# A two-block transformer forward on one core: activation tiles 512 columns apart, working-area regions at multiples of 128 columns

## The reference, cut to what matters

```python
def reference(x, ctx, ...):
    for l in range(2):                                   # first block
        hx = modulate(rmsnorm(x, norm_w[l]), ...)
        hc = modulate(rmsnorm(xc, norm_w[l]), ...)
        px = split_proj(hx @ w_in[l])                    # 1024 x 11008
        pc = split_proj(hc @ w_in[l])                    # layer 1: only ret_k, ret_v, att_k, att_v
        # four branches: retention, short conv, conformer conv, windowed attention, each (256, 512)
        merged = sum(sigmoid(g) * (br @ w_branch[i]) for i, (g, br) in enumerate(...))
        x = x + gate_x * (merged @ w_out[l])             # and xc likewise in layer 0
    x = rmsnorm(x, final_norm_w)
    for i in range(2):                                   # second block
        h = rmsnorm_2(x, norm_g[i, 0]) * (1 + sc_m) + sh_m
        y = rglru_mixer(h, ...) if i == 0 else gla_mixer(h, ...)
        x = x + gt_m * rmsnorm_2(y, norm_g[i, 1])
        h = rmsnorm_2(x, norm_g[i, 2]) * (1 + sc_f) + sh_f
        u = causal_dwconv(h @ w_up[i], conv_w, conv_b)   # 1024 x 5632
        g, val = split(u)
        x = x + gt_f * rmsnorm_2((gelu(g) * val) @ w_down[i], norm_g[i, 3])
    return x
```

## Time and profile before

| | |
|---|---|
| median of three runs | 1770.68 us (1768.67 to 1771.08) |
| span of the profiled execution | 1766.0 us; 4.7 us less than the median, and no other time of this execution is on record |
| TensorE busy | 1717.7 us (97%) |
| VectorE busy | 1400.0 us (79%) |
| ScalarE busy | 873.9 us (49%) |
| HBM traffic over the span | 170 GB/s, 50.6% of the DMA engines' time |

### The profile page before, as it was taken

How to read it: one execution, slowest core, us unless ns; L and a number is a source line. 1 busy time by engine, 2 the same in 40 slices (tenths; PEclk the granted TensorE clock), 3 DMA queues, 4 the chain that set the end, 5 groups by cost and what they waited for, 6 DMA issues and landing times.

```text
span 1766.0 us, 29817 instructions
## 1 busy us (share of the span) xinstructions
PE 1717.7 (97%) x11416; PEld 1526.8 (86%) x11416; DVE 1400.0 (79%) x2572; ACT 873.9 (49%) x1542; POOL 0.2 (0%) x4
## 2 busy tenths in 40 slices
PE   6999999999999999999999999999999999999998
PEld 3788887777888888897988899999999999999998
DVE  7799996546789998888877699977888568778874
ACT  4222224456233233353346755577666547566553
POOL 0000000000000000000000000000000000000000
PEclk9999999999999999999999999999999999999999
DMA  9583211211767876744323289744455545345553
GB/s 342 203 282 118 85 63 49 96 37 37 253 224 244 276 243 215 238 144 143 120 96 101 94 307 320 252 156 156 160 190 172 189 135 159 115 143 192 191 173 114
DMA packets 242188, 301.42 MB, mean 171 GB/s; under 512 B 6000, under 2 KB 223472, under 8 KB 241664
## 3 DMA queue, kind: packets, MB, share of 16 engines
q1 hardware_dynamic: 242048, 299.52, 50.6%
HBM read 298.45 MB, written 1.05 MB: 170 GB/s over the span
## 4 chain that ended last, share of the span: by engine, by line
PE 46%; DVE 5%; ACT 3%; issue 2%; DVEq 0%; ACTq 0%
PE bank L667 10%; PE bank L662 10%; PE bank L664 10%; PE bank L1044 3%; PE bank L1045 3%; PE bank L1046 3%; ACT w_hi L1359 1%; DVE w_lo L2116 1%; PE bank L638 1%; PE bank L640 1%; PE bank L639 1%; PE bank L1109 1%; PE bank L1175 1%; PE bank L1014 1%; PE bank L1160 1%
## 5 line engine op out<-in xcount | busy, mean ns | idle before, releaser
L2116 DVE TENSOR_TENSOR w_lo<-ring,w_hi 128x1024 fp32r<-128x1024 f32 (+2 forms) x436 | 489.4, 1131 | 182.4 <-ACT w_hi L1359 181.0
L1359 ACT ACTIVATE w_hi<-ring 128x1024 fp32r<-128x1024 f32 (+2 forms) x436 | 423.7, 982 | 166.9 <-PE bank L667 99.4
L662 PE MATMUL bank<-h_hi,w_hi 128*128 128x256 f32 (+2 forms) x2142 | 386.6, 322 | 0.4
L667 PE MATMUL bank<-h_hi,w_lo 128*128 128x256 f32 (+2 forms) x2142 | 379.1, 319 | 0.1
L664 PE MATMUL bank<-h_lo,w_hi 128*128 128x256 f32 (+2 forms) x2142 | 379.0, 319 | 0.0
L662 PEld LDWEIGHTS bank<-h_hi,w_hi 128*128 128x128 f32 x2142 | 316.6, 189 | 35.5 <-issue 2.7
L667 PEld LDWEIGHTS bank<-h_hi,w_lo 128*128 128x128 f32 x2142 | 317.0, 188 | 30.1 <-DVE w_lo L2116 0.3
L664 PEld LDWEIGHTS bank<-h_lo,w_hi 128*128 128x128 f32 x2142 | 317.1, 188 | 29.9
L1345 ACT ACTIVATE work<-bank 128x512 f32<-128x512 f32 (+1 forms) x134 | 67.3, 521 | 255.8 <-PE bank L667 205.4
L1345 ACT ACTIVATE arena<-bank 128x256 f32<-128x256 f32 (+4 forms) x125 | 56.4, 454 | 205.3 <-PE bank L667 125.4
L2423 DVE SCALAR_TENSOR_TENSOR arena<-arena,params 128x512 f32<-128x512 f32 (+1 forms) x240 | 130.5, 612 | 0.0
(11 more groups left out here) (324 smaller groups left out, 2286.4 us busy)
## 6 DMA issues: line engine op xcount, KB each, us to landing
ring<-in_w_in SPq DMA_DIRECT2D x86, 1024.0 KB, 5.4
arena<-in_ada_w_t SPq DMA_DIRECT2D x96, 512.0 KB, 6.0
ring<-in_ffn_w_up SPq DMA_DIRECT2D x44, 1024.0 KB, 5.0
ring<-in_w_branch SPq DMA_DIRECT2D x32, 512.0 KB, 4.7
arena<-in_w_mod_t SPq DMA_DIRECT2D x32, 512.0 KB, 5.3
ring<-in_ffn_w_down SPq DMA_DIRECT2D x16, 1024.0 KB, 5.1
ring<-in_gla_w_in SPq DMA_DIRECT2D x12, 1024.0 KB, 5.2
ring<-in_w_out SPq DMA_DIRECT2D x8, 1024.0 KB, 6.1
```

Of the source, the lines that this page charges most:

```text
L662: pe.matmul(out[:, 0:n], w[0][:, k, :], hi(k, n), start=k == 0, stop=False)
L667: m = pe.matmul(out[:, 0:n], w[1][:, k, :], hi(k, n), start=False, stop=k == tiles - 1)
L1359: nc.scalar.activation(w_hi[u % PARTS][:, 0:src.shape[1], :], src, ACT.Copy)\
L2116: step(nc.vector.tensor_tensor(w_lo[u % PARTS][:, 0:nk, :], src, w_hi[u % PARTS][:, 0:nk, :].bitcast(F32), ALU.subtract), f"lo {u}", *(["u ...
```

## The change

The tiles of h_hi and h_lo are 512 columns apart for every stage and start at column 0; both_hi and both_lo go away, because they are now the same as h_hi and h_lo. g_hi and g_lo start at column 0 of a tile and so reach two columns into the tile's second half; the merged sums of layer 1, which lay in that half, move to the arena (columns 0 and 6400). The arena regions that lay 16 columns short of a multiple of 128 (2288, 4336, ...) or 16 above one (16656) go to multiples of 128, x1_hi, x1_lo and the slots of the modulation blocks move by 16 columns, and the arena grows from 18,704 to 18,816 columns. The two h tensors shrink by 128 columns each, so that everything behind them lies up to 256 columns lower. On all engines the instructions stand in the same order with the same shapes, and the waits are the same; only addresses differ, and for the merged sums of layer 1 also the tensor.

```diff
--- before.py
+++ after.py
@@ -153,12 +153,10 @@
         params, tables = sbuf("params", N_PARAM), sbuf("tables", N_TABLE)
         xT = sbuf("xT", KT * 2 * S)[:].rearrange("p (t s) -> p t s", t=KT)
 
-        h_parts = [sbuf(n, KT * (2 * S + 16), F32R)[:].rearrange("p (t s) -> p t s", t=KT) for n in ("h_hi", "h_lo")]
-        h_hi, h_lo = (h[:, :, 16:16 + 2 * S] for h in h_parts)
-        g_hi, g_lo = (h[:, :, 14:14 + LATE_N] for h in h_parts)
-        both_hi, both_lo = (h.rearrange("p t s -> p (t s)")[:, 0:KT * 2 * S].rearrange("p (t s) -> p t s", t=KT)
-                            for h in h_parts)
-        in_hi, in_lo = (both_hi, h_hi), (both_lo, h_lo)
+        h_parts = [sbuf(n, KT * 2 * S, F32R)[:].rearrange("p (t s) -> p t s", t=KT) for n in ("h_hi", "h_lo")]
+        h_hi, h_lo = h_parts
+        g_hi, g_lo = (h[:, :, 0:LATE_N] for h in h_parts)
+        in_hi, in_lo = (h_hi, h_hi), (h_lo, h_lo)
 
         w_parts = [sbuf(n, PARTS * KT * P, F32R)[:].rearrange("p (u t n) -> p u t n", u=PARTS, t=KT) for n in ("w_hi", "w_lo")]
         w_hi, w_lo = ([w[:, i] for i in range(PARTS)] for w in w_parts)
@@ -190,7 +188,7 @@
         level = tables[:, at:at + LATE]
         gla_a = tables[0:16, at + LATE:at + LATE + 512]
 
-        arena_cols = 18704
+        arena_cols = 18816
 
         with nc.sbuf_tensor("arena", [P, arena_cols], F32) as arena:
             pass
@@ -214,33 +212,34 @@
         u_pad = carve(0, BT, 2, S + 2 * PAD), carve(BT * (S + 2), BT, 1, S + 2 * PAD)
         k_wt = [carve(1024 * i, ST, HEADS, P) for i in range(2)]
         att_o = carve(0, BT, 2 * S)
-        s_br = carve(2288, BT, 2 * S)
-        f_br = carve(4336, BT, 2 * S)
-        ret_q = ret_o = carve(6384, BT, 2 * S)
-        ret_k, ret_v = carve(8432, BT, 2 * S), carve(10480, 2 * ST, BW)
-        att_q = carve(12528, BT, 2 * S)
-        z_sil = dict(ret=carve(8432, BT, 2 * S), att=carve(10480, BT, 2 * S), cf=carve(12528, BT, 2 * S))
-        merged = carve(8432, KT, 2 * S)
-        att_k, att_ks = carve(14576, 2 * S), carve(15088, 2 * S)
-        att_v = carve(15600, 2 * ST, P)
-        state = carve(16112, HEADS, 2, P)
+        s_br = carve(2304, BT, 2 * S)
+        f_br = carve(4352, BT, 2 * S)
+        ret_q = ret_o = carve(6400, BT, 2 * S)
+        ret_k, ret_v = carve(8448, BT, 2 * S), carve(10496, 2 * ST, BW)
+        att_q = carve(12544, BT, 2 * S)
+        z_sil = dict(ret=carve(8448, BT, 2 * S), att=carve(10496, BT, 2 * S), cf=carve(12544, BT, 2 * S))
+        merged = carve(8448, KT, 2 * S)
+        att_k, att_ks = carve(14592, 2 * S), carve(15104, 2 * S)
+        att_v = carve(15616, 2 * ST, P)
+        state = carve(16128, HEADS, 2, P)
         branch = dict(ret=ret_o, sc=s_br, cf=f_br, att=att_o)
 
         def merged_part(l, lo, k):
 
             if l:
-                return (h_lo if lo else h_hi)[:, k, S:2 * S]
+                at = (0, 6400)[k // 4] + 2 * S * (k % 4) + S * lo
+                return arena_r[:, at:at + S]
             if k < 6:
-                at = (0, 2288, 6384)[k // 2] + 4 * S * (k % 2) + 2 * S * lo
+                at = (0, 2304, 6400)[k // 2] + 4 * S * (k % 2) + 2 * S * lo
                 return arena_r[:, at:at + 2 * S]
-            return (both_lo if lo else both_hi)[:, k, :]
+            return (h_lo if lo else h_hi)[:, k, :]
 
 
         def parts_of(at):
             return arena_r[:, at:at + BT * 2 * S].rearrange("p (t s) -> p t s", t=BT)
 
-        branch_hi = parts_of(16656)
-        z_sil["sc"] = carve(16656, BT, 2 * S)
+        branch_hi = parts_of(16768)
+        z_sil["sc"] = carve(16768, BT, 2 * S)
 
         def z_part(l, a, n):
 
@@ -248,7 +247,7 @@
                 return z_sil[a][:, n, :]
             return f_br[:, n, S:2 * S] if a == "sc" else z_sil[a][:, n, 0:S]
 
-        branch_lo = dict(ret=parts_of(6384), sc=parts_of(2288), cf=parts_of(4336), att=parts_of(0))
+        branch_lo = dict(ret=parts_of(6400), sc=parts_of(2304), cf=parts_of(4352), att=parts_of(0))
 
         def merged_tile(l, n):
 
@@ -263,7 +262,7 @@
             return early_gate(m) if l and m < EARLY_GATES else act_t[m % 4][:, 0:2 * S if l == 0 else S]
 
         x1_hi, x1_lo = (arena_r[:, c:c + KT * LATE_N].rearrange("p (t s) -> p t s", t=KT)
-                        for c in (8432, 8432 + KT * LATE_N))
+                        for c in (8448, 8448 + KT * LATE_N))
 
         def row_of(i):
 
@@ -456,7 +455,7 @@
         mod_slot_of = {m: i for i, m in enumerate(mod_order)}
 
         def mod_slot(m):
-            return carve(12560 + D * (mod_slot_of[m] % MOD_SLOTS), D)
+            return carve(12576 + D * (mod_slot_of[m] % MOD_SLOTS), D)
 
         def mod_in(m):
 
@@ -1483,7 +1482,7 @@
                     split_to(2)
                     shift_row(1)
                     shift_col(1)
-                    modulated("n1 0", (0, 1), lambda k, g: mod1[0][:, k, g:g + 1], start_shift, both_hi)
+                    modulated("n1 0", (0, 1), lambda k, g: mod1[0][:, k, g:g + 1], start_shift, h_hi)
                 if l:
                     act.wait_ge(shapes_landed, 32)
 
@@ -2247,7 +2246,7 @@
                     dve.wait_ge(x_landed, 32)
                     inverse("n1 0", 2 * S)
                     tile, low = normed("n1 0", (0, 1), lambda k, g: gain1[0][:, k, g:g + 1], lambda k, g: mod1[0][:, k, g:g + 1],
-                                      both_hi, both_lo)
+                                      h_hi, h_lo)
                     after(f"start mod {START + 1}")
                     modulation1(0, 0, 4)
                     split_to(1)
```

## The result

The changed kernel took 1775.84 us (median of five runs, 1775.33 to 1777.55), the kernel before 1768.74 us beside it (five runs, 1767.47 to 1771.08). That is 1.0040 of the time before, interval 1.0028 to 1.0052: 7.1 us slower. The forecast was 1779.5 us against a median before of 1770.68, so +8.9. Three of the five runs before are those that the prediction had; two more brought their median from 1770.68 to 1768.74.

A forecast was written before the change was run, and what follows sets the result against it. TensorE's matmul pace, set by operand addresses, was taken as the bound. 11.9 + 1.8 - 3.8 - 1.0 = +8.9 us gave a forecast of 1779.5 us, range 1766 to 1785.

The forecast's parts named there:

- 256 columns, streamed and down with h: Projections, 4,752 matmuls, 117.5 to 120.0 ns, +11.9 us; down projections with h stationary, 1,056, 118.3 to 120.0, +1.8 us.
- 512 columns: Arena matmuls in layer 0, 231.3 to 226.8 ns; layer 1's early tiles, 231.9 to 226.8; together -3.8 us.
- 258 columns: Late stages, 312 matmuls whose offsets change: -1.2 to +0.8 us, taken as 0.
- absorbed by waits: TensorE's two waits for a weight tile's high part absorb 0 to 4.3 us of the loss; 1.0 taken.
- the first witness: Down projection's middle part with arena operands, already at offset 0: 33 matmuls of 256 columns at 120.0 ns each.
- the second: Low part of att_o at offset 0: four matmuls at 117.5 ns, after eight at offset 16 at 113.8.
- the fast pace: 256 columns at 113.8 ns, seen in eight matmuls at offset 16 and lost within four at offset 0.
- 256 columns find the fast pace: Rival: 256 columns settle near 113.8 ns at offset 0, 26 us gained, 1744 us; chance 0.11.
- half of it: Rival: pace wanders after stalls, short groups stay near 118.7 ns, +2.7 us, 1773 us; chance 0.09.
- the 312 matmuls of one group: The 258-column matmuls (104 x 3) in late stages; each could gain 3.7 ns or lose 2.5.
- the waits for w_hi: TensorE's waits for a weight tile's high part, 1.7 and 2.6 us, where part of the loss might be absorbed.
- The 4.7 us between them: Median 1770.68 us above the profiled span of 1766.0; added to the predicted span 1774.9 to give 1779.6.

The follow-up runs named there:

- experiment 1: Matmuls alone in place of the whole computation, start column and tile distance varied, two orders: 256 columns 119.9 ns at offset 0, 113.3 and 117.9 at 16.
- experiment 4: Matmuls alone again, 256 columns at every fourth offset, 512 at every eighth, weights also starting at 16 or 48: 113.3 to 120.0 ns for 256 columns.
- experiment 5: Changed kernel with h 48 columns later from layer 1 on, ff_hi and ff_lo from 9808, merged sums partly from 6448: 1759.25 us, ratio 0.9942.
- the arena alone: Kernel before with only the arena's regions moved to multiples of 128 and 2 KB less scratch: 1767.12 us, ratio 0.9994 (0.9985 to 1.0002).

## Why the prediction was right

Direction, mechanism and most of the size were right. The 11,416 matmuls stand in the same order in both traces, so each one's distance to the next can be compared one by one. The sums over the span, beside the terms predicted (where a matmul belongs to a pace and where to a wait is a choice that moves some tenths of a microsecond between rows):

| term | predicted | measured |
|---|---|---|
| 256 columns, streamed and down with h | +11.9 +1.8 = +13.7 | +12.45 (6,079 matmuls) |
| 512 columns | -3.8 | -3.58 |
| 258 columns | 0 (-1.2 to +0.8) | +0.30 |
| absorbed by waits | -1.0 (0 to 4.3) | -0.68 |
| plain float32 matmuls | not named | -0.49 |
| stretches at half clock, with the waits they shorten | not named | +1.78 |
| sum over the span | +8.9 | +9.7 |

- **256 columns.** The pace at offset 0 is 120.0 wherever it settles, as the first witness had it; the second had shown only that the fast pace is lost there. The term is 1.2 us too large because the pace before was not 117.5 everywhere: its mean over all was 117.86 and after it 119.91, and the 6,079 include the 288 of the down projection's arena part, which had 120.0 before as after (eight stretches of 36, not of 39). The rival "256 columns find the fast pace" fell (120.0, never 113), and so did "half of it" (113.8 became 120.0 in the merge). The first witness streams its operand in two pieces and the second had only four matmuls, at 117.5 and not yet at 120.0, so neither proved the pace of a projection; that they held was partly luck. The runs bear them out afterwards: in experiments 1 and 4 offset 0 had one pace in every series (120.0 and 226.7), where 16 and 48 had two, and experiment 5 shows that the two-piece stream follows its offset too.
- **The word "offset".** That it is the difference of the two operands' columns, and not one operand's column, was assumed; experiment 4 shows it (both at 16 or at 48 runs as both at 0). That it counts modulo 128 was wrong: modulo 64. It changed nothing here, since 112 and 16 and 0 are told apart by both.
- **512 columns.** All three places came to 226.7; -3.58 against -3.8.
- **258 columns.** 120.15 to 120.68 ns, +0.30 us, inside the bounds, though these were worked out for the 312 matmuls of one group, and the trace has 576: those of the other lines and those from the arena were left out.
- **Absorbed.** Little, as said, but elsewhere: not at the waits for w_hi, which hardly moved, but before output tiles in layer 1's early projections, where the loop of ScalarE and VectorE sets the cadence (an output tile every 3.15 us in both kernels). From 768 to 800 us both kernels went through the same matmuls in 32.0 us, though those of 256 columns had gone from 117.9 to 119.7 ns. One wait grew (0.98 to 1.43 us before the last merged sums).
- **Not foreseen: stretches at half clock.** One window of 4 us in the kernel before, at 1.00 (it had 1.00 from 802 to 806 us as well), and two in the changed one and in the one with the arena alone:

```profile
41.00:45.00 4.00, 4.00 (x19) 2.54 (x18) 2.81 (x6) 2.65 (x5) 0.00 (x0) 1.00 1.10 351
```

```profile
41.00:45.00 4.00, 4.00 (x13) 3.06 (x11) 2.81 (x6) 2.63 (x5) 0.00 (x0) 0.59 1.10 353
802.00:806.00 4.00, 4.00 (x12) 3.17 (x11) 4.00 (x10) 0.00 (x0) 0.00 (x0) 0.57 0.05 12
```

```profile
41.00:45.00 4.00, 4.00 (x16) 2.55 (x15) 3.37 (x6) 1.40 (x3) 0.00 (x0) 0.83 1.09 353
802.00:806.00 4.00, 4.00 (x16) 3.17 (x15) 4.00 (x9) 0.00 (x0) 0.00 (x0) 0.81 0.39 89
```

The mean granted clock is 0.59 and 0.57, the 1.2 GHz level for most of the window, and 13 matmuls run where 19 did at 1.00. Before the second, TensorE had waited 1.9 us. It is not the change's doing as far as shown: the kernel with the arena alone, with h as before and no slower than before, has such stretches in the same two places. They cost the profiled execution 1.8 us net: a wait of TensorE at 60 us became 1.3 us shorter, which gave back most of the 1.6 that the first one had cost. Every run has a mean granted clock on record, and these speak for chance: 0.997 in the profiled execution of the kernel before, but 0.994 to 0.997 in 16 later runs of it, only three of them at 0.997; 0.995 and 0.996 in the five runs of the changed kernel.
- **From the span to the median.** The 4.7 us between them were carried over as they stood, and this step was wrong. Every run on record with both has 1.8 us between time and span (1777.55 and 1775.7 for the profiled one of the changed kernel). So the profiled execution of the kernel before was one of about 1767.8 us, 2.9 faster than the median that stood beside it, and these 2.9 are the larger part of the forecast's 3.7 us too much. The same explains 9.7 in the spans against 7.1 in the medians: the changed kernel's profiled execution was the slowest of its five (1775.7, their median span 1774.1), and that of the kernel before lay 0.9 us below its own median. The terms that the forecast named came to +8.5 against its +8.9; that this is so near is in part luck, because the first was 1.2 too large and the others together 0.8 too small. The other 1.3 us of the spans are terms that it didn't name.

The Trainium skill was weighed in the prediction: by "SBUF — State Buffer", section "SBUF: two separate sides", TensorE never waits on anyone, and by "TensorE: Matmul & The Clock Gate", section "Step-by-step: what each phase is for", loading the next weights takes nothing from the running matmul. By the prediction's reading of these, addresses would cost nothing. The runs disagree with that reading: in experiment 1 TensorE was alone (ScalarE's busy share 1%), and one form had 113.3 and 120.0 ns by the start column alone. Whether it is the weights' load that costs the running matmul its time, no run here shows.

## What to carry to other kernels

Read the pace as the distance of starts, place by place, before trusting a mean: a difference of 2 to 6 ns between places with one instruction form is worth asking for the addresses behind it. "Aligned" is not "fast": the difference between the streamed operand's first column and that of the weights loaded meanwhile decides, and the best value depends on the number of columns (0 for 512, 28 for 256 in one piece here). Series of a few dozen matmuls find candidates, but two are not enough: offset 48 had 113.3 in both of its first series and 117.8 in the next two. Then look for the pace in the kernel itself, place by place: a stream in two pieces gained at 48 and not at 28. Before counting a faster pace as a gain, look for stages in which the start of an output tile is given by other engines; there it buys nothing.

## What was new about the hardware

- One float32r matmul of 256 columns takes 113.3 to 120.0 ns between starts, and one of 512 226.7 to 234, by the difference of operand columns modulo 64, at one granted clock. The best values, 113.3 and 226.7, are 272 and 544 periods of a 2.4 GHz clock, 17/16 of one period per column; 120.0 is 288.
- Several offsets have more than one pace (4, 16 and 48 with 113.3 as one of them; 8, 20, 32 and 40 less far apart). Which one a series takes differed between orders, between executions, and between stages of one execution. The kernels with h at 16 or 48 had runs up to 10 us apart, which would fit; two traces show the two paces in the feed-forwards. What decides it stays open.
- 128 and 384 columns showed no such effect at the offsets tried (111.7 and 173.3 ns). Why the period is 64 columns, and whether it is the reading of the weights that meets the reading of the streamed operand, was not shown.
